# Filler work of a chunk loop in another order, and half a weight slab more of it inside the loop

## The reference

```
u, v, q, k, vv, o, gates = split_proj(modulate(x, sh1, sc1) @ w_in)          # latent
u_c, v_c, ... = split_proj(modulate(ctx, csh1, csc1) @ w_in)                 # 256 context tokens
h = mlstm_bidirectional(context inputs, latent inputs)                       # 4 heads, chunkwise
    # per chunk: scores = (q k^T) * w_intra ; num = scores v + w_inter * (q C) ; den likewise
    #            h = num / max(|den|, exp(-m)) ; C, n, m carried to the next chunk
y_a = u * (w_s mixed over (layer_norm(v) * g + b) + b_s)                     # spatial gating
y_b = head_norm(h) * hn_g * sigmoid(o)
y = concat(y_a, y_b) @ w_out
```

## Time and profile before

| | |
|---|---|
| time, median of 3 runs | 3580.67 us (3579.88 to 3581.6) |
| the profiled execution, its own time | 3580.04 us |
| its span in the trace | 3578.3 us |
| mean granted TensorE clock | 0.991 |
| PE busy | 3495.5 us, 98% |
| DVE busy | 2518.0 us, 70% |
| ACT busy | 1457.7 us, 41% |
| chunk loop of the third block, first inter to last intra | 2602.78 to 2726.68 us of the span |

### The profile page before, as it was taken

One profiled execution on the slowest core, in us unless ns is written; L12 is line 12 of the kernel. 1 busy time (PEld: TensorE's weight loads), 2 busy tenths in 40 slices (PEclk: granted clock), 3 DMA queues, 4 the chain that ended last, 5 costly groups with the idle time before them and its releaser, 6 DMA issues. The chain is left out here.

```text
span 3578.3 us, 43299 instructions
## 1 busy us (share of the span) xinstructions
PE 3495.5 (98%) x16868; PEld 2851.2 (80%) x16868; DVE 2518.0 (70%) x3407; ACT 1457.7 (41%) x2057; POOL 300.2 (8%) x305
## 2 busy tenths in 40 slices
PE   8999999999999999999999999999999999999998
PEld 7977877888887887667787888876987768888887
DVE  5487588888886897453557776656547477888895
ACT  3345363333344422542533333326322266773123
POOL 0000012222222001230000000012000000000000
PEclk9999999999999999999999999999999999999999
DMA  3102111111121112111213322231121213667651
GB/s 132 48 1 103 39 42 53 53 53 54 53 82 72 65 54 54 41 74 52 77 59 98 106 101 100 100 133 60 55 69 53 83 48 147 241 247 290 246 205 59
DMA packets 112558, 331.27 MB, mean 93 GB/s; under 512 B 18349, under 2 KB 33325, under 8 KB 103778
## 3 DMA queue, kind: packets, MB, share of 16 engines
q1 hardware_dynamic: 112354, 328.51, 26.1%
HBM read 253.82 MB, written 66.13 MB: 89 GB/s over the span
## 5 line engine op out<-in xcount | busy, mean ns | idle before, releaser
L2814 DVE TENSOR_TENSOR residual<-residual,psum 128x512 f32<-128x512 f32 x224 | 150.3, 685 | 70.3 <-PE psum L2362 70.3
L2360 PE MATMUL psum<-parts_r 128*128 128x512 f32 x448 | 177.5, 396 | 3.5 <-DVE parts_r L2804 3.5
L2362 PE MATMUL psum<-parts_r 128*128 128x512 f32 x448 | 175.3, 391 | 0.0
L2361 PE MATMUL psum<-parts_r 128*128 128x512 f32 x448 | 175.3, 391 | 0.0
L3844 DVE SCALAR_TENSOR_TENSOR residual<-psum,ada,residual 128x512 f32<-128x512 f32 x192 | 137.9, 746 | 37.7 <-PE psum L3395 19.8
L1759 DVE TENSOR_TENSOR residual<-residual,psum 128x512 f32<-128x512 f32 x256 | 160.2, 681 | 0.0
L4243 DVE SCALAR_TENSOR_TENSOR mixer<-scratch,params,mixer 128x1024 f32<-128x1024 f32 x120 | 156.8, 1306 | 4.0
L1317 PE MATMUL psum<-mixer_r,parts_r 128*128 128x512 f32 x304 | 118.4, 389 | 0.7 <-ACT rows L1439 0.7
L1319 PE MATMUL psum<-mixer_r,parts_r 128*128 128x512 f32 x304 | 118.3, 389 | 0.0
L1318 PE MATMUL psum<-gemm_input_r,parts_r 128*128 128x512 f32 x304 | 118.3, 389 | 0.0
L3538 ACT ACTIVATE parts_r<-parts 128x1792 fp32r<-128x1792 f32 x24 | 40.9, 1705 | 180.3 <-DVE parts L3828 180.3
(11 more groups left out here) (947 smaller groups left out, 10849.9 us busy)
## 6 DMA issues: line engine op xcount, KB each, us to landing
y_blocks<-parts_r SPq DMA_DIRECT2D x84, 512.0 KB, 3.4
parts<-in_w SPq DMA_DIRECT2D x15, 1024.0 KB, 4.8
parts<-in_w_down SPq DMA_DIRECT2D x14, 1024.0 KB, 4.9
parts<-in_w_up SPq DMA_DIRECT2D x13, 1024.0 KB, 4.9
masks<-in_w_ada SPq DMA_DIRECT2D x48, 256.0 KB, 2.9
rows<-in_w_ada SPq DMA_DIRECT2D x48, 256.0 KB, 3.1
mixer_r<-y_blocks SPq DMA_DIRECT2D x12, 1024.0 KB, 9.6
low_r<-y_blocks SPq DMA_DIRECT2D x12, 1024.0 KB, 12.2
```

What stands on the lines that cost most here:

```text
L2360: pe.matmul(bank, w_high[:, kd, at], high[:, 2 * kd + n, :], start=start, stop=False, skip_group_check=True)
L2361: pe.matmul(bank, w_low[:, kd, at], high[:, 2 * kd + n, :], start=False, stop=False, skip_group_check=True)
L2362: return pe.matmul(bank, w_high[:, kd, at], low[:, 2 * kd + n, :], start=False, stop=stop, skip_group_check=True)
L2814: dve.tensor_tensor(x, x, ps, ALU.add).then_inc(drained, 1)
```

## The change

The fillers are now in a table, `beside`: v1 in steps 0, 1, 4 and 5, o1 in 2 and 3, o0 in 6 and 7, o2 in 8 and 9, o3 in 10 and 11, and the first tile of u0, now a slab of its own (`u0a`), in 12 and 13. Steps 14 and 15 have none. Both calls of `constant_products` around there are gone. Behind the loop PE does the two units of the second tile (`u0b`), then two u1 units, then `spatial(0..3)`, then the transposes. u0a's results go to a scratch tile, `first_u`, and `gate_u` reads them there. The splits of o2, o3, u0a and u0b lie at the end of DVE's iterations 7, 8, 11 and 14, and the split of u1 lies between `normal_v(3)` and `normal_v(4)`.

```diff
+    beside = {0: [("v1", 0), ("v1", 1)], 1: [("v1", 2), ("v1", 3)], 2: [("o1", 0, 0)], 3: [("o1", 0, 1)],
+              4: [("v1", 4), ("v1", 5)], 5: [("v1", 6), ("v1", 7)], 6: [("o0", 0, 0)], 7: [("o0", 0, 1)],
+              8: [("o2", 0, 0)], 9: [("o2", 0, 1)], 10: [("o3", 0, 0)], 11: [("o3", 0, 1)],
+              12: [("u0a", 0, 0)], 13: [("u0a", 0, 1)]}
...
@@ sync @@
             for j in range(2, 16):
                 rows_in(j)
-                if j == 9:
+                if j == 7:
                     sp.wait_ge(products, done_at["v1", 7])
                     load("o2")
                     load("o3")
-            sp.wait_ge(products, done_at["o3", 0, 1])
-            load("u0")
+                if j == 11:
+                    sp.wait_ge(products, done_at["o2", 0, 1])
+                    load("u0a")
+                if j == 13:
+                    sp.wait_ge(products, done_at["o3", 0, 1])
+                    load("u0b")
@@ tensor @@
-                elif 9 <= j < 13:
-                    if j == 9:
-                        c.constant_products(pe, PS[:, 7, :], 18)
-                    unit(("o2", "o3")[(j - 9) // 2], 0, (j - 9) % 2)
+                if len(mine) == 2:
+                    piece(*mine[1])
+                elif mine:
+                    unit(*mine[0])
...
-            c.constant_products(pe, PS[:, 0, :], 8)
-            for m in range(2):
-                for n in range(2):
-                    unit("u0", m, n)
+            for n in range(2):
+                unit("u0b", 0, n)
+            for n in range(2):
+                unit("u1", 0, n)
             pe.wait_ge(tables_landed, 48)
             pe.wait_ge(v_step, 24)
             for g in range(4):
                 spatial(g)
-            for n in range(2):
-                unit("u1", 0, n)
             transposes(range(0, 4))
@@ scalar @@
             for j in range(16):
                 if j == 1:
                     round_slab("o1")
-                if j == 9:
-                    round_slab("o2")
-                    round_slab("o3")
                 if j < 15:
                     weights(j + 1)
+                if j == 13:
+                    round_slab("u0b")
+                for u in beside.get(j, []):
+                    ... (evacuates the step's filler)
+                if j == 7:
+                    round_slab("o2")
+                    round_slab("o3")
+                if j == 11:
+                    round_slab("u0a")
@@ vector @@
                 if j < 13:
                     keys(5 + j)
-                if j == 9:
+                if j == 7:
                     split_slab("o2")
-                if j == 10:
+                if j == 8:
                     split_slab("o3")
+                if j == 11:
+                    split_slab("u0a")
+                if j == 14:
+                    split_slab("u0b")
                 if 10 <= j < 12:
                     for t in range(4 * j - 40, 4 * j - 36):
                         dve.wait_ge(drained, done_at["v1", t])
                         dve.bn_stats(stats[:, t, :], v[:, t, :]).then_inc(stats_done, 1)
...
-            split_slab("u0")
             output(15)
             for t in range(8):
                 normal_v(t)
+                if t == 3:
+                    split_slab("u1")
...
                 dve.tensor_tensor(h_groups, h_groups, bc(mean), ALU.subtract).then_inc(n_step, 1)
-            split_slab("u1")
```

More of the change, by code:

```diff
@@ L5134, in block3_mixer @@
     FIRST = len(units)
-    units += [("o0", 0, 0), ("o0", 0, 1), ("o1", 0, 0), ("o1", 0, 1)] + [("v1", t) for t in range(NC_)]
-    units += [("o2", 0, 0), ("o2", 0, 1), ("o3", 0, 0), ("o3", 0, 1)]
+    beside = {0: [("v1", 0), ("v1", 1)], 1: [("v1", 2), ("v1", 3)], 2: [("o1", 0, 0)], 3: [("o1", 0, 1)],
[3 rows of a table added]
+    units += [u for j in range(14) for u in beside[j]]
     SECOND = len(units)
-    units += [(w, m, n) for w in ("u0", "u1") for m in range(2) for n in range(2)]
+    units += [("u0b", 0, 0), ("u0b", 0, 1)] + [("u1", m, n) for m in range(2) for n in range(2)]
     done_at = counted(units)
-    mixed_bank = lambda g: 2 + g if g < 4 else (7, 6, 0, 1)[(SECOND + g) % 4]
+    first_u = c.T[:, 0, :]
+    mixed_bank = lambda g: 2 + g if g < 4 else (7, 6, 0, 1)[(SECOND + g - 2) % 4]
     LAST = (4, 6, 5, 7)
@@ L5167, in block3_mixer @@
         late = counted(["v1", "o0", "o1"])
-        soon = {w: i for i, w in enumerate(("q", "k", "vals0", "vals1", "v0", "o2", "o3", "u0", "u1"), 1)}
+        soon = {w: i for i, w in enumerate(("q", "k", "vals0", "vals1", "v0", "o2", "o3", "u0a", "u0b", "u1"), 1)}
         gb_landed, wq_landed = [gb_landed_0, gb_landed_1], [wq_landed_0, wq_landed_1]
@@ L5230, in _ @@
             load("u1")
-            sp.wait_ge(products, done_at["u0", 1, 1])
+            sp.wait_ge(products, done_at["u0b", 0, 1])
             if prefetch:
@@ L5659, in _ @@
                     act.activation(rstd[:, 0:8], rstd[:, 0:8], ACT.Exp, scale=-0.5).then_inc(rstd_done, 1)
-            round_slab("u0")
             act.wait_ge(out_step, 16)
             round_slab("u1")
-            for m in range(2):
-                for n in range(2):
-                    evacuate(("u0", m, n), M[:, 4 + m, halves[n]])
+            for n in range(2):
+                evacuate(("u0b", 0, n), M[:, 5, halves[n]])
+            for n in range(2):
+                evacuate(("u1", 0, n), M[:, 6, halves[n]])
             act.wait_ge(n_step, 3)
@@ L5672, in _ @@
             act.activation(M[:, 8:12, :], M[:, 8:12, :], ACT.Sigmoid).then_inc(o_done, 1)
-            for n in range(2):
-                evacuate(("u1", 0, n), M[:, 6, halves[n]])
             if prefetch:
@@ L5922, in _ @@
                 gate_u(g)
-    for slot, n in enumerate((6, 4, 2, 1)):
+    for slot, n in enumerate((6, 4, 2, 2)):
         c.loads[slot] += 16 * n
```

50 lines of the change are left out of this document (24 added, 26 removed).

## The result

| | before | changed |
|---|---|---|
| time, median | 3576.53 us (3568.99 to 3583.38, 9 runs) | 3586.12 us (3581.77 to 3592.47, 9 runs) |
| the profiled execution, its own time | 3580.04 us | 3585.31 us |
| its span | 3578.3 us | 3583.6 us |
| PE busy | 3495.5 us | 3487.3 us |
| mean granted TensorE clock | 0.991 | 0.991 |

The account below looks back on a forecast made before the run. PE (98% busy) bound the kernel before; afterwards DVE's chain behind the loop binds. 9.3 + 2.7 in the loop less 5.0 behind gives +7.0 on 3580.04; with 0.6 for the median and 0.4 for clock, 3588.1 us; range 3581.5 to 3593.

Parts of the forecast that it names:

- The split behind ACT's rounding, step 8: At intra(8), PE stalls 2.3 us because DVE's split of o2 waits for ACT's rounding, with weigh(8) behind it.
- The same in step 12, with the statistics: At intra(12), u0a's split waits likewise and four statistics stand ahead of weigh(12); PE stalls 4.7 us.
- L: End of the loop's last intra; forecast 12.0 us later, at 2738.65, with steps 14 and 15 about 4.3 us.
- S: Landmark: start of inter(8), the start of step 8, taken as 2672.95 and unmoved by the reordering of steps 0 to 7.
- a short fall of the clock: Half clock behind PE waits: 2.7 us lost in step 12 and again at the transposes, 0 in step 8.
- DVE's chain: DVE's serial work behind the loop, output(15) to gate_u: as long as before, 2.2 us added by u1's split, starting 12.0 us later.
- PE's wait ahead of the transposes: Behind spatial, PE waits for DVE's gate_u, at least 5.9 us (6 to 10 expected), with half clock behind it.
- T: Landmark: start of the second transposes, right behind the last u1 unit; forecast at 2797.05, against 2790.05 before.
- The sum, +7.0: Whole change to the last u1 unit's end: 9.3 + 2.7 us in the loop, -5.0 behind it.
- Rival 2: Behind the loop, PE goes on binding at the first transposes; faster, total 3573 to 3577; chance 0.06.
- Rival 1: In the loop, stalls are smaller while DVE's chain still binds behind it; without stalls and clock loss 3578.0; chance 0.10.
- rival 3: More waits: late rows for argument(8), clock drop in step 8 or longer low clock; +10 to +14 us; chance 0.14.

Follow-up runs that it names:

- `e1_round_early`: Changed kernel with ScalarE's roundings of o2, o3 and u0a moved ahead of the evacuation of that step's filler; 3580.52 us, ratio 1.0009 against the kernel before.
- `e3_split_back`: `e2_order_back` with u1's split also put back behind the head norm's mean subtraction on VectorE; 3590.04 us, ratio 1.0044 against the kernel before.
- `e6_v_norm_early`: Changed kernel with early roundings, u1's units and split put back, v's statistics and normalisations moved into the loop; 3569.23 us, ratio 0.9977 against the kernel before.
- `e8_before_v_early`: Kernel before with v's statistics one iteration earlier and two of eight normalisations moved into the loop; 3574.57 us, ratio 0.9996 against the kernel before.
- `e2_order_back`: Changed kernel with u1's first two units and their evacuation put back between spatial and the transposes; 3594.27 us, ratio 1.0053 against the kernel before.
- `e7_constants`: Changed kernel with 30 constant products in PE's wait ahead of the transposes; 3588.32 us, ratio 1.0033 against the kernel before.
- `e4_u0a_behind`: Changed kernel with u0a's two units taken out of steps 12 and 13 and put behind the loop; 3587.03 us, ratio 1.0038 against the kernel before.

## Why the prediction was right

The forecast was 3588.1, with 0.53 on slower; it came out 3586.12 and slower. That "slower" owes something to luck: by the forecast's own bound of 3587.8 the time would have been no change, and it is slower because the kernel before came out at 3576.53 and not at the 3580.67 that the bound stood on. The mechanism is settled by the runs, and the terms stand so:

- **The split behind ACT's rounding, step 8: 2.3 us.** Measured 2.25, 2.26. `e1_round_early` takes away only ACT's order, and the wait is gone. The Trainium skill, "TensorE: Matmul & The Clock Gate", section on the array's architectural detail, calls ACT and DVE strict FIFO. The rows agree: `weigh(8)`, whose inputs were ready, started 1.14 us behind the split, never ahead of it (2672.77, 2673.91).
- **The same in step 12, with the statistics: 4.7 us.** Measured 4.63.
- **L.** From S the forecast was 65.7 us, and it was 66.48, 65.29 and 66.49. Mis-sized inside: steps 14 and 15 took 4.50 us instead of 4.3, since they kept a wait of 0.45 us, put down to `weigh(15)`, where 0.1 was taken; a short fall of the clock costs 1.5 us where 2.7 were taken from block two; and it fell in step 8 as well, in two of three executions. The prediction reasoned from one row that a gap of 2.7 us keeps the clock up and so gave step 8 nothing (with 0.4 for the chance). That row was one draw. These errors nearly cancel.
- **DVE's chain: `gate_u` at L + 41.7.** Measured L + 42.24. The missing 0.5 is at its start: `output(15)` began 0.63 us behind L (2738.20), where 0.1 was taken, since `output(14)` stood ahead of it. The 2.2 us for u1's split is shown by `e3_split_back`. u1's first unit waited 1.66 us for it, where 1 was taken.
- **PE's wait ahead of the transposes: at least 5.9, 6 to 10 us.** Measured 8.19, released by `gate_u`. From the start of `gate_u` to T 16.7 us were forecast and 15.10 measured: the low clock costs 1.6 us there, not 2.7, and the transposes end 0.5 us sooner than the 3.0 taken.
- **The sum, +7.0.** S to T gives 123.5 less 116.4, +7.0 on the mean of three executions. The exact match is partly chance: in the first pair alone it is +6.7 by S, and +4.9 by the span's own clock, since S came 1.9 us earlier; over all pairs S to T gives +5.1 to +9.3, as much scatter as the terms in dispute. To the end of the last constants it is +6.5.
- **Rival 2, that PE goes on binding behind the loop,** had its condition right: `gate_u` ending within about 34 us of L. No run of the changed order meets it. `e6_v_norm_early` does, at L + 24.9, and is faster than both; `e8_before_v_early` shows that before the change DVE's chain is not the bound. Rival 1 fell with step 8's 2.25. Of rival 3 the fall of the clock in step 8 took place, for 1.5 us where it counted 2.7; the rows for argument(8) were not late, and its +10 or more did not come.

What stays open: the medians differ by 9.6 us (0.19 to 0.39%, 6.8 to 14 us), the spans by 6.7. The unprofiled runs of before lie some 3 us below its profiled ones, those of the changed kernel less than 1 below theirs. The four medians of before themselves lie between 3575.93 and 3578.49. The traces don't cover unprofiled runs, so up to 3 us of the difference are not attributed. The forecast of 3588.1 stood on a median of 3580.67 before; the later runs gave 3576.53, so the centre was about right in level partly by chance: +7.4 was forecast, +9.6 came.

## What to carry to other kernels

When work is moved into a loop, look at what it stands in front of on each in-order engine: a split that waits for a rounding, behind an evacuation, behind a filler, cost 10.1 us up to the loop's end here, clock included, and three roundings moved on ScalarE took it back, 7.0 us of it as far as the end of the stage. Work of the loop's own engine moved in (two units of 5.66 us) gains nothing if another engine's serial chain behind the loop sets the end; shorten that chain in the same edit, and check that the engine is then not early for something else (a 9.33 us wait ahead of `spatial` cost 7.5 us more by the stage's end than one of 8.19 behind it). Where single executions scatter by 6 us in untouched code, measure a stretch from a common landmark and repeat the profile before a term of 1 to 3 us is believed.

## What was not expected of the hardware

- **Half clock under steady work.** In `e2_order_back` PE was busy 15.72 of 15.72 us at a granted clock of 0.50, from its wait to the end of `spatial`. The Trainium skill, "TensorE: Matmul & The Clock Gate", section on the clock gate, ties the clock to how busy the engine has been. By that alone it should have risen within this stretch; it rose only in the 512-column matmuls of u1. Here the measurement decides: `spatial`'s matmuls (one-row products of 512 columns and small ones of 128, all float32) did not bring the clock back, and in `e7_constants` it rose 1.7 us into `constant_products` (1.00 from 2777.9). The clock also fell inside `spatial` with no wait at hand: in the changed kernel at 2766.8, when PE had worked since 2750.12. The second four `spatial` show it in every trace: in all thirteen the clock falls within them and comes back only in the constants behind, up to 13.7 us later. But `e4_u0a_behind` ran its first four at full clock throughout (2763.08 to 2771.6). Why, no run here tells.
- **The same wait, two clocks.** 2.25 and 2.26 us in step 8 lowered the clock in two of three executions of one kernel, and in four of the seven traces with this wait; the 4.6 us of step 12 lowered it in all seven. In the third execution of before, waits of 0.98, 1.25 and 1.15 us in the bare steps 14 and 15 were followed by half clock too (2729.0 to 2732.3), in the first two they were not.
- **Scatter upstream.** The start of step 8 lay between 2668.92 and 2675.16 us over thirteen traces, and the stretch behind T took 14.74 to 19.56 us, longer where more low clock fell on it.
